# Down projection: matmul columns read and written alternating between the halves of a product, in groups of 16 and of 8

## The reference

```
D_MODEL, SEQ = 2048, 256
D_FF = 5632
h = rms_norm(h_state, norm_ffn_pre) * (1.0 + sc2) + sh2
y = (silu(h @ ffn_w_gate) * (h @ ffn_w_up)) @ ffn_w_down     # (256, 5632) @ (5632, 2048)
h_state = h_state + g2 * rms_norm(y, norm_ffn_post)
```

## Time and profile before

| | |
|---|---|
| median of 3 runs | 1748.32 us (1743.9 to 1748.74) |
| the profiled execution: its own time | 1750.69 us |
| the profiled execution: span from first to last instruction | 1749.0 us |
| PE busy | 98% of the span, 7837 matmuls |
| DVE, ACT, POOL busy | 57%, 42%, 9% |
| mean granted TensorE clock | 0.994 of full speed |
| down projection, blocks 0 to 3 | 60.76, 59.84, 59.84, 60.00 us |

### The profile page before, as it was taken

How to read it: one execution, slowest core, us unless ns; L and a number is a source line. 1 busy time by engine, 2 the same in 40 slices (tenths; PEclk the granted TensorE clock), 3 DMA queues, 4 the chain that set the end, 5 groups by cost and what they waited for, 6 DMA issues and landing times.

```text
span 1749.0 us, 21470 instructions
## 1 busy us (share of the span) xinstructions
PE 1710.9 (98%) x7837; PEld 1381.1 (79%) x7837; DVE 995.1 (57%) x1097; ACT 742.3 (42%) x833; POOL 160.5 (9%) x176
## 2 busy tenths in 40 slices
PE   6999999999999999999999999999999999999998
PEld 2458887788878888888888778888888888888886
DVE  2446666667765776676665555444544554444444
ACT  3323222226656454445454574444444444443442
POOL 0011000000036354230000000000000000000000
PEclk8999999999999999999999999999999999999999
DMA  9999998889989576665777566666666666766662
GB/s 366 364 380 339 349 330 318 325 321 326 323 326 287 170 227 189 178 193 192 236 223 256 169 206 189 187 189 191 189 186 190 191 187 189 261 193 193 194 194 93
DMA packets 183834, 420.07 MB, mean 240 GB/s; under 512 B 12896, under 2 KB 13248, under 8 KB 173920
## 3 DMA queue, kind: packets, MB, share of 16 engines
q1 hardware_dynamic: 158464, 308.34, 55.2%
q10 hardware_dynamic: 17968, 82.49, 12.9%
q0 software_dynamic: 7344, 28.46, 4.9%
HBM read 398.74 MB, written 20.50 MB: 240 GB/s over the span
## 4 chain that ended last, share of the span: by engine, by line
PE 84%; DMA 8%; DVE 4%; issue 1%; ACT 1%; ACTq 1%; SPq 0%; DVEq 0%; POOLq 0%; POOL 0%
PE ps L1511 24%; PE ps L1499 24%; PE ps L1503 24%; DMA wm<-in_w_mod 7%; PE ps L1581 2%; DVE acc L1015 2%; PE ps L1555 2%; DMA raw<-in_w_mod 1%; PE ps L1597 1%; PE ps L1785 1%; PE ps L1801 1%; PE ps L1839 1%; ACTq L626 1%; PE ps L1756 1%; PE ps L1662 0%
## 5 line engine op out<-in xcount | busy, mean ns | idle before, releaser
L1003 DVE TENSOR_TENSOR w_lo<-raw,w_hi 128x1024 fp32r<-128x1024 f32 x496 | 612.0, 1237 | 522.5 <-ACT w_hi L613 522.4
L613 ACT ACTIVATE w_hi<-raw 128x1024 fp32r<-128x1024 f32 x496 | 524.1, 1060 | 788.2 <-PE ps L1511 635.8
L1499 PE MATMUL ps<-w_hi,h_hi 128*128 128x512 f32 x1472 | 465.9, 396 | 2.0 <-DVE h_lo L1405 2.0
L1503 PE MATMUL ps<-w_hi,h_lo 128*128 128x512 f32 x1472 | 457.5, 390 | 0.0
L1511 PE MATMUL ps<-w_lo,h_hi 128*128 128x512 f32 x1472 | 402.5, 390 | 5.4 <-DVE w_lo L1003 5.4
L1511 PEld LDWEIGHTS ps<-w_lo,h_hi 128*128 128x128 f32 x1472 | 276.7, 188 | 64.2 <-DVE w_lo L1003 6.3
L1503 PEld LDWEIGHTS ps<-w_hi,h_lo 128*128 128x128 f32 x1472 | 277.0, 188 | 58.0
L1499 PEld LDWEIGHTS ps<-w_hi,h_hi 128*128 128x128 f32 x1472 | 273.4, 188 | 58.4 <-DVE h_lo L1405 2.6
L1015 DVE SCALAR_TENSOR_TENSOR acc<-wm,csil,acc 128x2048 f32<-128x2048 f32 x60 | 141.0, 2351 | 78.8 <-DMA wm<-in_w_mod 78.8
L1499 PE MATMUL ps<-w_hi,hid_hi 128*128 128x512 f32 x352 | 109.7, 389 | 0.0
L1503 PE MATMUL ps<-w_hi,hid_lo 128*128 128x512 f32 x352 | 109.7, 389 | 0.0
(11 more groups left out here) (292 smaller groups left out, 1349.2 us busy)
## 6 DMA issues: line engine op xcount, KB each, us to landing
raw<-in_w_in SPq DMA_DIRECT2D x184, 512.0 KB, 6.5
wm<-in_w_mod ACTq DMA_DIRECT2D x64, 1024.0 KB, 7.2
raw<-in_ffn_w_gate SPq DMA_DIRECT2D x88, 512.0 KB, 4.4
raw<-in_ffn_w_up SPq DMA_DIRECT2D x88, 512.0 KB, 4.3
raw<-in_ffn_w_down SPq DMA_DIRECT2D x88, 512.0 KB, 4.7
raw<-in_w_mod SPq DMA_DIRECT2D x64, 512.0 KB, 8.0
raw<-in_w_out SPq DMA_DIRECT2D x32, 512.0 KB, 4.8
px<-stage ACTq DMA_DIRECT2D x44, 256.0 KB, 6.6
```

Of the source, the lines that this page charges most:

```text
L613: act.activation(w_hi[:, j % SPLIT, :, :], raw[:, j % RAW, :, :], ACT.Copy).then_inc(w_high, 1)
L1003: dve.tensor_tensor(w_lo[:, j % SPLIT, :, :], raw[:, j % RAW, :, :], w_hi[:, j % SPLIT, :, :].bitcast(F32), ALU.subtract).then_inc(w_low, 1)
L1499: pe.matmul(o, hi[:, kk, c], w_hi[:, q, e, :], start=kk == 0, stop=False)
L1503: pe.matmul(o, lo[:, kk, c], w_hi[:, q, e, :], start=False, stop=False)
```

## The change

`products` takes one more argument, `weave`. With 1 the matmuls are as before. With 16 or 8 both the moving operand and the output of each of its 12 matmuls are read and written through another access pattern: the 512 columns are seen as two halves of 256, and the pattern takes a group of `weave` columns of the first half, then the group at the same place of the second half, and so on. With 16 there are 32 groups (16 in each half), with 8 there are 64 groups. Operand and output take the same order, so every column of the weights still lands in its own place of the bank, and every other engine finds its data where it was. The number of matmuls, their columns, their order and all waits stay as they are. `WEAVE` gives 1 to block 0, 16 to block 1, 8 to block 2, and 1 to the first 18 slots of block 3; the second loop of block 3 keeps the default of 1. All other callers of `products` keep the default too.

```
+WEAVE = (1, 16, 8, 1)
...
-            def products(s, j, k, last_k, tiles, first_bank, between=None, used=1, signal=w_used):
+            def woven(t, parts):
+
+                return t if parts == 1 else t.rearrange("p (a b c) -> p b a c", a=2, c=parts)
+
+            def products(s, j, k, last_k, tiles, first_bank, between=None, used=1, signal=w_used, weave=1):
...
-                        o = bank(first_bank + n)
+                        o = woven(bank(first_bank + n), weave)
                         kk, c = k + e, slice(m * P, (m + 1) * P)
-                        pe.matmul(o, hi[:, kk, c], w_hi[:, q, e, :], start=kk == 0, stop=False)
+                        pe.matmul(o, hi[:, kk, c], woven(w_hi[:, q, e, :], weave), start=kk == 0, stop=False)
...
-                        pe.matmul(o, lo[:, kk, c], w_hi[:, q, e, :], start=False, stop=False)
+                        pe.matmul(o, lo[:, kk, c], woven(w_hi[:, q, e, :], weave), start=False, stop=False)
...
-                        last = pe.matmul(o, hi[:, kk, c], w_lo[:, q, e, :], start=False, stop=kk == last_k)
+                        last = pe.matmul(o, hi[:, kk, c], woven(w_lo[:, q, e, :], weave), start=False, stop=kk == last_k)
...
-                    products(S_DOWN + n * DOWN_SLOTS, j, 2 * j, D_FF // P - 1, HID, 2 * (1 - n % 2))
+                    products(S_DOWN + n * DOWN_SLOTS, j, 2 * j, D_FF // P - 1, HID, 2 * (1 - n % 2),
+                             weave=WEAVE[n])
```

## The result

The changed kernel takes 1753.69 us (median of 5 runs, 1752.52 to 1757.01) against 1746.26 for the kernel before in the same comparison (5 runs, 1743.90 to 1748.74). The ratio is 1.004, with a 95% interval of 1.0026 to 1.0054: slower by 4.5 to 9.4 us. The forecast was no change.

The account below looks back on a forecast made before the run. The prediction took PE's matmul stream alone to bound blocks 1 and 2. Its terms, 264 x 0 + 264 x 0 = 0, left the median unchanged at 1748.3 us, with range 1741 to 1762 (0.80).

Parts of the forecast that it names:

- What bounds the two blocks: Blocks 1 and 2: PE's matmul stream alone, 226.7 ns per matmul, 59.84 us per block; ACT and DVE only follow.
- The output: PSUM writes in blocks 1 and 2: taken as 0, bounded by 0 and 204 ns more per matmul.
- rival 3: Both blocks: broken output slows PSUM's accumulation to the float32 rate, 108 us more, 1856 us; chance 0.05.
- The moving operand, groups of 16: Block 1's reads: each packet of 16 columns stays one unbroken run, so 0; bounds 13.3 ns less to 14.2 more.
- Groups of 8: Block 2's reads, a packet spanning two groups: taken as 0; if packets end at jumps, 13.3 or 226.7 ns more.
- rival 2: Both blocks: each jump costs one column's time, 0.44 ns, together 11.2 us, 1759.5 us; chance 0.12.
- Rival 1: Block 2 alone: a packet ends at a jump; 59.8 us at full price (chance 0.13), 3.5 us at small (0.08).
- rival 4: Both blocks: alternating between places 1 KB apart removes the surplus clock, at most 7.0 us faster, 1741.3 us; chance 0.10.
- The view behind it: PE's stream goes in packets of 16 columns, 17 clocks or 7.08 ns each; a started packet costs nearly a full one.
- The DVE row: DVE's exponent instructions, groups of 1, 2, 4, 8, take 284 to 290 ns regardless: speaks for free jumps, no proof.

Follow-up runs that it names:

- repeat: Changed kernel with plain writes, moving operand one short stretch read over and over: 256 columns twice 2.72 us a slot, 32 sixteen times 2.84, 16 thirty-two times 2.88.

## Why the prediction was wrong

**What bounds the two blocks** was right. PE's stream alone sets them, ACT and DVE follow, and each ns on a matmul went into the time 264 times per block.

**The output** was right: 0. Its upper bound and rival 3, the float32 rate, are refuted by the run that keeps only the writes.

**The moving operand, groups of 16** is the step that failed first. It took 0, because "the packets are the same", out of a range of -13.3 to +14.2 ns. The runs show +13.3 ns, close to the upper bound. **Groups of 8**: also 0, out of 0 to 226.7; the runs show +16.7 ns, 3.3 more than groups of 16. The sum should have been 264 x (13.3 + 16.7) = 7.9 us instead of 0.

**The rivals.** The sign and the places are those of rival 2, a price in both blocks, but not its law. It had the second excess double the first and 11.2 us in all; the second is only a quarter larger. Its bound of one column's time per jump was met by groups of 16 (32 clocks for 32 groups) and by chance only: groups of 8 pay 40 clocks for 64, groups of 4 56 for 128, groups of 32 24 for 16, groups of 64 none, and groups of 2, after the transposes, 244 for 256. Rival 1 put the price in block 2 alone and is refuted by block 1, rival 4 by both; in no run did matmuls of 512 columns come closer than 226.7 ns over a slot.

**The view behind it** was wrong too. From three widths the prediction made a rule, one clock in 16 columns with a last packet paid in full. Its own reservation, that the 258 column matmuls load 128 columns of weights and those of 256 only 64, was the truth. Three rows that differed in two things were read as if they differed in one. The view that the surplus was a steady rate made a free jump look natural. The duration, which the prediction trusted more than the distance, misled the same way: in the run with the shorter matmuls 256 and 258 columns both last 283 ns with 128 columns of weights, and 256 columns last 276 with 64.

**The DVE row** did not carry over. DVE reads groups of 1, 2, 4 and 8 at one speed, at under a number per ns; PE's read of fp32r wants more than two per ns (512 in 226.7 ns), and pays for groups of up to 32. The reservation was written down and given too little weight.

**What stays open** is the law of the price. Shown is that for groups of 8, 16 and 32 it arises in reading the moving operand; that it is there without a far place (repeat) and with half the weights; that groups of 64 and of 128 are free between the halves; and that it does not add to the disturbance by a shifted stationary piece. Not shown is why 8 costs hardly more than 16, why the four quarters are cheaper than the halves (2.77 against 2.88 and 2.92), and why one pattern ran at 3.00 and then at 2.80 us a slot and another at 4.08 and then at 3.94. What such a jump costs therefore hangs on something besides the pattern, and the values here are those of this stream.

## What to carry to other kernels

Keep the moving operand of fp32r matmuls in aligned runs, of at least 64 columns (256 bytes) as far as was tried: with 512 columns and 128 wide weights that is 226.7 ns, groups of 32 to 8 cost 10 to 17 ns more between halves and 4 to 13 round four or eight pieces, groups of 2, with both sides broken up, over 100. The output may be permuted freely in groups of 8 or 16, so where one side has to be broken up, let it be the output. A row on a slower engine is no evidence that a faster one has slack, and before a rule is made out of rows of different widths, list everything else in which those rows differ.

## What the runs showed of the hardware beyond that

The distance of plain matmuls depends on the weight load beside them. With 512 columns it is 226.7 ns for an aligned stationary piece 128 wide, 230.0 for 96 and for 64, 231.7 for 32, and 231.1 and 232.5 for 128 wide shifted by 16 and by 4 columns; with 256 columns 120.0 ns for 128 wide and 113.3 for 64. Narrower weights can make a matmul faster or slower. A start of the moving operand 8, 32 or 96 bytes off costs 6 to 7 ns, 16 bytes 5 and 64 bytes 2. The page "SBUF — State Buffer" of the Trainium skill (Specifications) gives lines of 16 bytes, of which at least two hits each are needed for full bandwidth, and a penalty for each change to a new line. Groups of 8 and 16 columns, if the rows start on a line, fill every line that they touch and change lines no more often than the plain read. Broken up in the read alone they took 243.3 and 240.0 ns instead of 226.7, so that rule is not enough for this stream.
